# Two wide state steps on DVE and the sum of weights on POOL in a hybrid SSD, attention and Hyena kernel

## The reference, cut to what matters

```
# SSD, for each direction, chunk by chunk
decay = exp(where(tri, la[l] - la[s], -inf))           # 128 x 128 for each head
w = (C B^T) * decay * dt                                # weights inside the chunk
y = w x + (C h) * exp(la)                               # inside, and carried in
h = h * exp(la[-1]) + B^T (to_end * x)                  # the step of the state
# attention, for each head
attn = softmax(q0 k0) - lam * softmax(q1 k1)
```

## Time and profile before

| | |
|---|---|
| median of 3 runs | 3881.94 us (3874.04 to 3882.35) |
| the profiled execution | 3885.88 us, span 3884.1 us |
| busy share of the span | PE 87%, DVE 64%, ACT 28%, POOL 27% |
| granted clock of PE, mean | 0.949 of full speed |

### The profile page before, as it was taken

One profiled execution on the slowest core, in us unless ns is written; L12 is line 12 of the kernel. 1 busy time (PEld: TensorE's weight loads), 2 busy tenths in 40 slices (PEclk: granted clock), 3 DMA queues, 4 the chain that ended last, 5 costly groups with the idle time before them and its releaser, 6 DMA issues. The chain is left out here.

```text
span 3884.1 us, 48584 instructions
## 1 busy us (share of the span) xinstructions
PE 3384.3 (87%) x18212; PEld 2751.6 (71%) x18212; DVE 2470.1 (64%) x4480; ACT 1093.9 (28%) x1981; POOL 1067.4 (27%) x782
## 2 busy tenths in 40 slices
PE   6999999999868886886997899999999688858798
PEld 2787888888757775554783577888887587745477
DVE  4134577755369996885664324657775599968765
ACT  2111222212245454332210211222211455523321
POOL 4233334333212321210222423433433022232121
PEclk8999999999989998998998899999999799979899
DMA  5254223223173312344435155323322633133442
GB/s 208 65 155 147 80 91 96 86 89 97 53 204 98 84 58 71 118 113 132 146 97 206 58 122 174 99 78 103 95 90 62 199 90 93 43 107 110 128 143 69
DMA packets 414893, 423.34 MB, mean 109 GB/s; under 512 B 57040, under 2 KB 351440, under 8 KB 413506
## 3 DMA queue, kind: packets, MB, share of 16 engines
q1 hardware_dynamic: 368676, 315.22, 28.2%
q10 hardware_dynamic: 45984, 105.01, 7.7%
HBM read 287.76 MB, written 124.01 MB: 106 GB/s over the span
## 5 line engine op out<-in xcount | busy, mean ns | idle before, releaser
L754 PE MATMUL l_p_acc<-l_u_hi,l_w_hi 128*128 128x512 f32 (+1 forms) x2208 | 605.7, 376 | 22.8 <-PEq L158 9.0
L754 PE MATMUL l_p_acc<-l_u_hi,l_w_lo 128*128 128x512 f32 (+1 forms) x2208 | 587.3, 367 | 0.0
L754 PE MATMUL l_p_acc<-l_u_lo,l_w_hi 128*128 128x512 f32 (+1 forms) x2208 | 586.7, 367 | 0.0
L754 PEld LDWEIGHTS l_p_acc<-l_u_hi,l_w_hi 128*128 128x128 f32 x2208 | 383.8, 189 | 99.2 <-issue 25.2
L667 POOL TENSOR_TENSOR l_w_hi<-l_wt,l_p_zero 128x1024 fp32r<-128x1024 f32 x100 | 200.5, 2005 | 899.7 <-PE l_p_acc L754 744.1
L754 PEld LDWEIGHTS l_p_acc<-l_u_lo,l_w_hi 128*128 128x128 f32 x2208 | 380.8, 189 | 71.7
L754 PEld LDWEIGHTS l_p_acc<-l_u_hi,l_w_lo 128*128 128x128 f32 x2208 | 380.5, 189 | 71.6
L1506 PE MATMUL l_at_pS<-l_at_k_hi,l_at_q 128*128 128x512 f32 (+1 forms) x400 | 166.6, 416 | 133.1 <-ACT l_at_prob L1622 75.6
L669 POOL TENSOR_TENSOR l_w_lo<-l_wt,l_w_hi 128x1024 fp32r<-128x1024 f32 x100 | 265.3, 2653 | 7.8
L1740 DVE TENSOR_REDUCE l_at_nmax<-l_at_pS 128x1 f32<-128x1280 f32 (+1 forms) x144 | 197.4, 1371 | 103.0 <-PE l_at_pS L1507 99.0
L2457 PE MATMUL l_o_pA<-l_o_w_hi,l_o_o_hi 128*128 128x512 f32 x576 | 223.7, 407 | 42.7 <-DVE l_o_o_lo L2567 31.6
(11 more groups left out here) (331 smaller groups left out, 7058.5 us busy)
## 6 DMA issues: line engine op xcount, KB each, us to landing
l_wt<-w_in SPq DMA_DIRECT2D x104, 512.0 KB, 3.9
l_n_wa<-w_ada SPq DMA_DIRECT2D x10, 2048.0 KB, 16.5
kf_d<-l_p_R SPq DMA_DIRECT2D x72, 256.0 KB, 3.6
xbc_d<-l_p_fin ACTq DMA_DIRECT2D x28, 640.0 KB, 2.9
l_at_K<-kf_d SPq DMA_DIRECT2D x64, 256.0 KB, 2.9
l_o_rows<-w_out SPq DMA_DIRECT2D x32, 512.0 KB, 4.9
l_o_oT<-o_d SPq DMA_DIRECT2D x16, 1024.0 KB, 7.0
qk_d<-l_p_late ACTq DMA_DIRECT2D x12, 1280.0 KB, 4.6
```

The costliest lines, as they stand in the source:

```text
L754: mm = pe.matmul(acc[:, a:a + w], (w_hi, w_lo)[wp][m % 2][:, k], (u_hi, u_lo)[up][:, k, t0 + c:t0 + c + w], start=(k == n == 0), stop=(k = ...
```

## The change

Three things. In `ssd_stage` POOL adds the two directions' exponentials (`sum_directions`), between the two chunks that it prepares in a tick. DVE makes both directions' states in two wide operations: a product of old states and decays into a new tile `kept`, and an addition of `pS`; the layout of `mine` is turned, so that `pick` is three copies, and the decays of both directions are picked by one slice with a step. In `combine` the `tensor_scalar` becomes a `scalar_tensor_tensor`.

```diff
-                    dve.tensor_scalar(back[:, s:s + 1], back[:, s:s + 1], sums[:, n % 4, 0:1], lam[:, 0:1], ALU.mult, ALU.mult).then_inc(mix_step, 1)
+                    dve.scalar_tensor_tensor(back[:, s:s + 1], back[:, s:s + 1], lam[:, 0:1], sums[:, n % 4, 0:1], ALU.mult, ALU.mult).then_inc(mix_step, 1)
...
-        mine = sb(nc, ctx, tag + "mine", [P, 2, 3, TT, 2, HPG])
+        mine = sb(nc, ctx, tag + "mine", [P, 2, 3, 2, TT, HPG])
+        kept = sb(nc, ctx, tag + "kept", [P, 2, HPG, HD])
...
+                def sum_directions(n):
+                    pool.wait_ge(exped, 2 * n + 2)
+                    pool.tensor_tensor(seg[:, n % 2, 0], seg[:, n % 2, 0], seg[:, n % 2, 1], ALU.add).then_inc(seg_summed, 1)
...
-                    for p in preps(j) if g < GROUPS else []:
-                        prep(g, p)
+                    n = tick - NO + 1
+                    todo = preps(j) if g < GROUPS else []
+                    if todo:
+                        prep(g, todo[0])
+                    if 0 <= n < NO * GROUPS:
+                        sum_directions(n)
+                    if len(todo) > 1:
+                        prep(g, todo[1])
...
-                    dve.tensor_copy(mine[:, g % 2].rearrange("p k t d h -> p (k t) d h"), cols).then_inc(picked, 1)
+                    for k in range(3):
+                        cols = small[:, k].rearrange("p t (d h) -> p d t h", d=2)[:, :, :, HPG * g:HPG * (g + 1)]
+                        dve.tensor_copy(mine[:, g % 2, k], cols).then_inc(picked, 1)
...
-                    dve.wait_ge(state_mm, at + 1)
-                    for h in range(HPG):
-                        last = dve.scalar_tensor_tensor(state[:, s, d, nxt, h], state[:, s, d, c, h], mine[:, s, 1, c, d, h:h + 1],
-                                                        pS[:, d * BANK + h * HD:d * BANK + (h + 1) * HD], ALU.mult, ALU.add)
-                    last.then_inc(state_ready, 1)
+                    decay = mine[:, s, 1].rearrange("p d t h -> p (d t) h")[:, both(c0, c1)].unsqueeze(3).to_broadcast([P, 2, HPG, HD])
+                    if at:
+                        dve.wait_ge(state_ready, 2 * at)
+                    dve.tensor_tensor(kept[:], states[:, both(c0, c1)], decay, ALU.mult).then_inc(decayed, 1)
+                    dve.wait_ge(decayed, at + 1)
+                    dve.wait_ge(state_mm, 2 * at + 2)
+                    new = pS[:, :].rearrange("p (d n) -> p d n", d=2)[:, :, 0:XG].rearrange("p d (h e) -> p d h e", h=HPG)
+                    dve.tensor_tensor(states[:, both(nxt0, nxt1)], kept[:], new, ALU.add).then_inc(state_ready, 2)
...
                 def weights(n):
-                    dve.wait_ge(exped, 2 * n + 2)
                     dve.wait_ge(cb_copied, n + 1)
                     both = seg[:, n % 2, 0]
-                    dve.tensor_tensor(both, both, seg[:, n % 2, 1], ALU.add).then_inc(seg_summed, 1)
                     dve.wait_ge(seg_summed, n + 1)
```

More of the change, by code:

```diff
@@ L1861, in ssd_stage @@
     with stage(nc, tag + "xc_in", tag + "xb0_in", tag + "xb1_in", tag + "o0_in", tag + "o1_in", tag + "o2_in", tag + "seg0_in", tag + "seg1_in", tag + "seg2_in", tag + "seg3_in", tag + "skip_in", tag + "sel_in",
-               tag + "zeroed", tag + "ones", tag + "built", tag + "picked", tag + "turned", tag + "x_copied", tag + "end_scaled", tag + "state_mm", tag + "state_ready",
+               tag + "zeroed", tag + "ones", tag + "built", tag + "decayed", tag + "picked", tag + "turned", tag + "x_copied", tag + "end_scaled", tag + "state_mm", tag + "state_ready",
                tag + "diffed", tag + "cb_mm", tag + "cb_copied", tag + "exped", tag + "seg_summed", tag + "u_split", tag + "u_mm", tag + "u_scaled", tag + "w_ready", tag + "y_mm", tag + "skipped", tag + "gated",
                tag + "stored0", tag + "stored1") as (ctx, sems):
-        (xc_in, xb0_in, xb1_in, o0_in, o1_in, o2_in, seg0_in, seg1_in, seg2_in, seg3_in, skip_in, sel_in, zeroed, ones, built, picked, turned, x_copied, end_scaled, state_mm, state_ready,
+        (xc_in, xb0_in, xb1_in, o0_in, o1_in, o2_in, seg0_in, seg1_in, seg2_in, seg3_in, skip_in, sel_in, zeroed, ones, built, decayed, picked, turned, x_copied, end_scaled, state_mm, state_ready,
          diffed, cb_mm, cb_copied, exped, seg_summed, u_split, u_mm, u_scaled, w_ready, y_mm, skipped, gated, stored0, stored1) = sems
@@ L2089, in prep @@
                     if p == 0:
-                        pool.wait_ge(picked, g + 1)
+                        pool.wait_ge(picked, 3 * (g + 1))
                         if g:
@@ L2094, in prep @@
                     x = tok[:, g % 2, c, 0:XG].rearrange("p (h e) -> p h e", h=HPG).unsqueeze(1).to_broadcast([P, 2, HPG, HD])
-                    pool.tensor_tensor(xend[:, c], x, mine[:, g % 2, 0, c].unsqueeze(3).to_broadcast([P, 2, HPG, HD]), ALU.mult).then_inc(end_scaled, 1)
+                    pool.tensor_tensor(xend[:, c], x, mine[:, g % 2, 0, :, c].unsqueeze(3).to_broadcast([P, 2, HPG, HD]), ALU.mult).then_inc(end_scaled, 1)
+                def sum_directions(n):
+                    pool.wait_ge(exped, 2 * n + 2)
+                    pool.tensor_tensor(seg[:, n % 2, 0], seg[:, n % 2, 0], seg[:, n % 2, 1], ALU.add).then_inc(seg_summed, 1)
                 pool.memset(seg_l[:].bitcast(F32), 1.0).then_inc(ones, 1)
@@ L2109, in pick, with both, step @@
                         dve.wait_ge(y_mm, NO * (g - 1))
-                    cols = small[:].rearrange("p k t (d h) -> p (k t) d h", d=2)[:, :, :, HPG * g:HPG * (g + 1)]
-                    dve.tensor_copy(mine[:, g % 2].rearrange("p k t d h -> p (k t) d h"), cols).then_inc(picked, 1)
[L2112 to L2118, removed]
-                    dve.wait_ge(state_mm, at + 1)
-                    for h in range(HPG):
-                        last = dve.scalar_tensor_tensor(state[:, s, d, nxt, h], state[:, s, d, c, h], mine[:, s, 1, c, d, h:h + 1],
-                                                        pS[:, d * BANK + h * HD:d * BANK + (h + 1) * HD], ALU.mult, ALU.add)
-                    last.then_inc(state_ready, 1)
+                    for k in range(3):
+                        cols = small[:, k].rearrange("p t (d h) -> p d t h", d=2)[:, :, :, HPG * g:HPG * (g + 1)]
+                        dve.tensor_copy(mine[:, g % 2, k], cols).then_inc(picked, 1)
+                    dve.wait_ge(picked, 3 * (g + 1))
+                def both(t0, t1):
+                    return slice(t0, TT + t1 + 1, TT + t1 - t0)
+                def step(g, k):
+                    (_, c0, nxt0), (_, c1, nxt1) = steps[2 * k:2 * k + 2]
+                    at, s = NSTEP * g + k, g % 2
+                    states = state[:, s].rearrange("p d t h e -> p (d t) h e")
+                    decay = mine[:, s, 1].rearrange("p d t h -> p (d t) h")[:, both(c0, c1)].unsqueeze(3).to_broadcast([P, 2, HPG, HD])
[6 more added lines that the diff above has]
+                    dve.tensor_tensor(states[:, both(nxt0, nxt1)], kept[:], new, ALU.add).then_inc(state_ready, 2)
                 def scale_carried(n):
@@ L2129, in scale_carried @@
                         dve.wait_ge(y_mm, n - 1)
-                    decay = mine[:, gr % 2, 2, outs[i]].rearrange("p d h -> p (d h)")
-                    dve.tensor_tensor(us[:, n % 2].rearrange("p d h e -> p (d h) e"), pU[:, :].rearrange("p (k e) -> p k e", e=HD),
-                                      decay.unsqueeze(2).to_broadcast([P, 2 * HPG, HD]), ALU.mult).then_inc(u_split, 1)
+                    decay = mine[:, gr % 2, 2, :, outs[i]].unsqueeze(3).to_broadcast([P, 2, HPG, HD])
+                    dve.tensor_tensor(us[:, n % 2], pU[:, :].rearrange("p (d h e) -> p d h e", d=2, h=HPG), decay, ALU.mult).then_inc(u_split, 1)
                     dve.wait_ge(u_split, n + 1)
@@ L2182, in _ @@
                     if g < GROUPS:
-                        for k in step_pairs(j):
-                            step(g, k)
+                        for k in step_pairs(j)[::2]:
+                            step(g, k // 2)
                     if 0 <= n - 1 < NO * GROUPS:
```

## The result

| | before | changed |
|---|---|---|
| median, us (runs) | 3882.14 (4) | 3911.95 (4) |
| lowest to highest | 3874.04 to 3888.24 | 3906.18 to 3920.93 |
| profiled execution, us | 3885.88 | 3920.93 |
| its span | 3884.1 | 3918.7 |
| state space stages, layer 0 and 1 | 247.4, 217.3 | 259.2, 233.5 |

The ratio is 1.0075 [1.0057, 1.0092]: slower, as forecast, but by 29.8 us where 14.0 were forecast, and outside the range of 3871 to 3908. The profiled spans differ by 34.6: 28.0 in the two state space stages, 2.8 in attention, 3.8 in the other stages, which are the same in all kernels here and took between 2530 and 2548 us in the profiled executions. The profiled execution of the changed kernel is the slowest of its four.

A forecast was written before the change was run, and what follows sets the result against it. TensorE (87% busy) and DVE (64%) were near their limit in the stages, DVE ending last in plain ticks. Terms 15.4 - 4.0 - 1.5 + 3.7 - 1.5 + 1.3 = +13.4, with attention +14.0 us: 3896.0, range 3871 to 3908.

The forecast's parts named there:

- preparation ticks: State space ticks (one output chunk each) with preparation: new product waits for POOL's second scaling, +0.64 us each, 24 ticks, +15.4.
- plain ticks: State space ticks with one step pair, no preparation: 5.39 and 3.98 us in turn instead of 4.90; 18 ticks, -4.0 us.
- last groups: Last group of each stage, 16 ticks without steps: DVE's L2134 waits for POOL's addition, +0.23 each, +3.7 us in all.
- second layer, last tick of a group: Three ticks with two step pairs, no preparation: 0.72 + 0.40 us saved, one collision of about 0.6, together -1.5 us.
- start of the stages, with their first two-pair tick: Stage's start, steps waiting for TensorE in turn, first addition, `pick` in three copies: +1.3 us, an allowance.
- attention: New operation in `combine`: one pointer scalar fewer saves 3.5 to 4.6 us, lost races with POOL up to +7; taken +0.6.
- Exclusion, and who waited first goes next: DVE operations with two SBUF inputs and POOL operations exclude each other whole; the first to wait goes next; product ends 0.55 behind.
- there are two pairs, with the same collision at the first: One in four ticks with preparation has two step pairs; it was counted at the same +0.64 us as the others.
- (1): Rival: contention does not bite, POOL's addition costs DVE nothing; about -21 us, 3861; chance 10%.
- (2): Rival: the new product goes in front of POOL's second scaling; about -9 us, 3873, faster; chance 15%.
- (4): Rival, middle: ticks without preparation and attention gain their best, the rest as forecast; +6.6 us, 3888.5, no measurable change; 15%.
- (3): Rival: more collisions, all 18 ticks without preparation at 5.2 us, attention +7; +30 at most, +24.5 at two thirds, 3906; 15%.

The follow-up runs named there:

- e5: Changed kernel plus five spare TensorE products, read by nobody, in the long wait of two-pair ticks with outputs: 3908.62 us against 3886.32, 1.0065.
- e3: Kernel before with only attention's `tensor_scalar` made a `scalar_tensor_tensor`; steps and addition as before: 3890.08 us, 1.0016.
- e1: Kernel before with only the addition of the two directions' exponentials moved to POOL; narrow steps and attention as before: 3874.46 us against 3886.27, 0.9971.
- e6: Changed kernel with the first pair's wide product made earlier, between the weights and the scaling of the carried part, where DVE idles: 3871.04 us, 0.9963.
- e10: Changed kernel with narrow steps at each stage's start, where no outputs lie beside them: 3914.33 us against 3884.0, 1.0079.
- e2: Kernel before with only the wide steps; exponentials added on DVE and attention as before: 3885.58 us, 1.0006.
- e4: Changed kernel with the addition of the two directions' exponentials left out on both engines, so weights are of one direction only: 3888.08 us, 1.0007.
- e7: Changed kernel with the first pair's wide product made early, the exponentials added on DVE again and attention as before: 3864.43 us, 0.9952.
- e8: Mixture: wide steps with early product only in ticks 2 to 4 of a group, POOL's addition only from the sixth tick, attention as before: 3872.55 us, 0.9972.
- e9: Mixture: early wide product in every tick with output, narrow steps at stage starts, POOL's addition in ticks 2 to 5, old attention: 3859.96 us against 3884.0, 0.9933.

## Why the forecast fell short

The direction and the mechanism held; in the profiled execution the size failed most by one term that was not in the sum, and less by small ones that came out higher. The changed kernel's ticks are set beside e5's, which has its chain without the fall of the clock.

| term | forecast | measured |
|---|---|---|
| preparation ticks, behind the first gate (22) | +14.1 | +13.5 |
| plain ticks (18) | -4.0 | -3.6 |
| last groups | +3.7 | +3.4 |
| second layer, last tick of a group (3) | -1.5 | +0.2 |
| group ends | -1.5 | -0.5 |
| start of the stages, with their first two-pair tick | +2.6 | +5.4 |
| PE at half clock behind the waits | no term | +9.6 |
| stages | +13.4 | +28.0 |
| attention | +0.6 | +2.8 in one execution, +0.7 in e3's |

*Exclusion, and who waited first goes next*: right. The product took 1.53 us beside the scaling, ended 0.54 behind it (0.55 forecast), and e1 and e6 show it from both sides: with a PSUM operand in that place (e1) or with the product elsewhere (e6) the wait is gone. Preparation ticks are 6.84 to 6.89 where +0.64 on 6.26 was forecast. *Plain ticks alternate*, 4.02 and 5.38 for 3.98 and 5.39: right, as is *the last group*, 4.54 for 4.53, though 14 of its 16 ticks are longer, not all.

*The step that failed* is the remark that in one of the four preparation ticks "there are two pairs, with the same collision at the first". For DVE it is true: in e5 the tick is 0.70 to 0.77 longer. But the second pair's products stand in front of TensorE's next work and wait for the first pair's states; that wait went from 1.30 to 2.76, and what TensorE did at full clock before it did in part at half clock after. I looked at the clock column of the earlier trace rows, saw 1.00, and took it for a constant of the stage. The price in the profiled execution, 9.6 us, is two thirds of the 14.6 that the forecast of its stages lacks.

How much of it is in the medians is not shown. The profiled execution has a mean granted clock of 0.945; the other three have 0.948 to 0.949, and the kernel before, in its executions, 0.946 to 0.952. The medians lack 15.8 us (29.8 less 14.0). With the clock held (e5) the kernel still loses 0.65%, about 22 to 25 us of the 29.8, so what is left of the miss lies in the other terms of the stages (18.4 in the table, where 13.4 was forecast), in attention, and in the spread of the runs.

*The start* was "an allowance", half of what it measured. Its steps wait for TensorE one after the other; a wide operation serves both directions at once, so TensorE can't begin one direction while DVE steps the other. On the timeline:

```profile
1562.05 1.10 PE L1970 MATMUL l_sd_pS<-l_sd_xend,l_sd_tok 128*128 128x256 f32 x4 [0.97 <-DVE l_sd_state L2142]
1564.12 1.10 PE L1970 MATMUL l_sd_pS<-l_sd_xend,l_sd_tok 128*128 128x256 f32 x4 [0.97 <-DVE l_sd_state L2142]
...
1570.37 0.69 DVE L2158 TENSOR_TENSOR l_sd_seg<-l_sd_seg,l_sd_cb 128x512 f32<-128x512 f32 x1 [1.91 <-POOL l_sd_seg L2100]
```

The pairs are 2.07 us apart, 1.78 with narrow steps (e10); a part of the 5.4 is also the first fall of the clock, at 1580.84, ahead of the first gate's end at 1584.62; and the first weights wait 1.91 us for POOL. The same serial order took the 1.5 us that I had set for the last tick of a group in the second layer, which also has two pairs: 6.77 in e5, 6.68 before. With the wide steps alone (e2) it is 6.82, with POOL's addition alone (e1) 6.13 to 6.22, so it is the wide form that costs there.

*Attention*: the new operation does take 0.22 instead of 0.27, and it does lose the race in the 13 units that I had counted as possible, so the sign is the unfavourable one: between +0.7 and +3.8 us by three comparisons, none of which fixes it better. The other traces agree on the sign: the two attention stages are 0.4 to 3.7 us longer in e3 and e4 than in e1 and e2, 1.7 to 2.3 in e5 and e6 than in e7 and e8, and 2.7 in e10 than in e9.

*The rivals*: (1) and (2) are refuted by the product's 1.53 us; (4) by the tick lengths. (3) came nearest in time, but not for its reason: plain ticks don't all collide. Its 3906 was the right neighbourhood from the wrong cause, and that its full sum, 14.0 + 9.4 + 6.4, is the measured 29.8 is chance.

## What to carry to other kernels

Before an operation is widened or moved between DVE and POOL, write down for each version whether both its inputs lie in SBUF, and what POOL has queued at that time: here each half of the step change was harmless alone and the pair was not, and moving one product into idle time (e6) turned +0.75% into -0.37%. Where a longer chain makes TensorE wait in an otherwise full stretch, look at the granted clock behind the longest wait, not at its mean, since the second cost can come near the first (here 9.6 us beside the 13.5 of the preparation ticks). Compare the mean clock of the other executions before that cost is taken for all of them. Spare products in that wait (e5) show within one run whether the clock is the cause.

## What the hardware showed that I had not expected

- A wait of 2.5 to 2.8 us of TensorE, in a stretch where it is busy 86% of the time (151.40 of 177 us), was followed in 16 of 18 places (changed kernel and e10) by a stretch at 1.2 GHz; one of 1.30 us never was. A wait of 1.93 us in the old steps (e3) was followed by one too.
- A DVE operation of one element for each partition, with two SBUF inputs, waits as long for POOL as a large one: 2.40 us instead of 0.22.
- POOL's addition gives way as well: its 72 run from 1.26 us to 1.70, and in the plain ticks which engine yields alternates from tick to tick without drifting.

```profile
L2100 POOL TENSOR_TENSOR l_sd_seg<-l_sd_seg x72: 1263/1270/1698, 1569.0 to 3689.5; 128x512 f32<-128x512 f32 x72
L2138 DVE TENSOR_TENSOR l_sd_kept<-l_sd_state,l_sd_mine x72: 677/756/1758, 1547.6 to 3656.0; 128x512 f32<-128x512 f32 x72
```
